# The first loads and constants of a decoder layer: two DMA queues, gains first, identity ahead of the zeroing

## What is computed

```python
def rms_norm(x, g):
    y = xf * lax.rsqrt(jnp.mean(xf * xf, axis=-1, keepdims=True) + EPS)
    return (y * g.astype(jnp.float32)).astype(x.dtype)

h = rms_norm(x, attn_norm_g)                 # x (1, 256, 2048)
proj = h @ w_in                              # (256, 11344)
(q_sb, k_sb, v_sb, q_ds, k_ds, v_ds, q_ix, k_ix, w_ix, g_sb, g_ds) = jnp.split(proj, IN_OFFSETS, axis=-1)
...                                          # two attentions, merged by gates
x = x + merged @ w_out
h = rms_norm(x, ffn_norm_g)
u = causal_depthwise_conv(h @ w_up, conv_w, conv_b)
gate, val = jnp.split(u, 2, axis=-1)
x = x + (jax.nn.silu(gate) * val) @ w_down
```

## Time and profile before

| | us |
|---|---|
| median of 3 runs | 1442.99 |
| lowest, highest | 1441.86, 1443.41 |
| the profiled execution, in all | 1443.47 |
| its span (first to last instruction) | 1441.7 |
| TensorE busy within the span | 1430.5 |
| VectorE, ACT, POOL busy | 1141.1, 841.9, 443.4 |

### The profile page before, as it was taken

How to read it: one execution, slowest core, us unless ns; L and a number is a source line. 1 busy time by engine, 2 the same in 40 slices (tenths; PEclk the granted TensorE clock), 3 DMA queues, 4 the chain that set the end, 5 groups by cost and what they waited for, 6 DMA issues and landing times.

```text
span 1441.7 us, 23615 instructions
## 1 busy us (share of the span) xinstructions
PE 1430.5 (99%) x7570; PEld 1224.0 (85%) x7570; DVE 1141.1 (79%) x1532; ACT 841.9 (58%) x1181; POOL 443.4 (31%) x487
## 2 busy tenths in 40 slices
PE   8999999999999999999999999999999999999999
PEld 7888888888888888888888888888888888788887
DVE  6778998986656556899967777778778778899988
ACT  6545677566767766666664555454554545465553
POOL 2310000423232213650015455755556555200000
PEclk9999999999999999999999999999999999999999
DMA  7555665655454545557555565555655565476564
GB/s 247 190 190 163 205 201 188 190 183 174 155 173 147 173 168 182 185 199 232 201 180 185 191 189 189 177 192 192 195 189 181 183 200 187 170 245 205 198 210 147
DMA packets 120535, 272.24 MB, mean 189 GB/s; under 512 B 10800, under 2 KB 10832, under 8 KB 120480
## 3 DMA queue, kind: packets, MB, share of 16 engines
q1 hardware_dynamic: 119424, 269.12, 56.9%
q0 software_dynamic: 736, 2.42, 0.6%
q10 hardware_dynamic: 320, 0.01, 0.0%
HBM read 269.42 MB, written 2.10 MB: 188 GB/s over the span
## 4 chain that ended last, share of the span: by engine, by line
PE 93%; DVE 3%; DMA 1%; issue 1%; POOL 1%; ACT 1%; DVEq 0%; ACTq 0%; POOLq 0%; SPq 0%
PE bank L2063 92%; DVE lo L1662 1%; DVE lo L1208 1%; PE bank L2112 1%; DMA raw<-in_w_out 0%; DMA raw<-in_w_down 0%; DMA rows_in<-in_attn_norm_g 0%; POOL u L2027 0%; ACT hi L719 0%; PE bank L2327 0%; PE bank L2368 0%; DVE conv L1614 0%; POOL conv L2030 0%; DVE y L1752 0%; DVE msum L1225 0%
## 5 line engine op out<-in xcount | busy, mean ns | idle before, releaser
L1099 DVE TENSOR_TENSOR lo<-raw,hi 128x1024 fp32r<-128x1024 f32 (+1 forms) x343 | 446.8, 1308 | 165.8 <-ACT hi L632 165.0
L632 ACT ACTIVATE hi<-raw 128x1024 fp32r<-128x1024 f32 (+1 forms) x343 | 360.1, 1053 | 271.6 <-PE bank L2063 267.5
L2063 PE MATMUL bank<-h2T,hi 128*128 128x512 f32 x1408 | 483.3, 394 | 0.0
L2063 PE MATMUL bank<-h2T,lo 128*128 128x256 f32 x1408 | 376.8, 278 | 0.0
L2063 PEld LDWEIGHTS bank<-h2T,hi 128*128 128x128 f32 x1408 | 257.9, 188 | 53.5
L2063 PE MATMUL bank<-hT,hi 128*128 128x512 f32 (+1 forms) x784 | 273.9, 396 | 0.0
L2063 PEld LDWEIGHTS bank<-h2T,lo 128*128 128x128 f32 x1408 | 264.4, 188 | 7.8
L2063 PE MATMUL bank<-hT,lo 128*128 128x256 f32 (+1 forms) x784 | 213.0, 282 | 0.0
L2027 POOL TENSOR_TENSOR u<-u,rms_row 128x256 f32<-128x256 f32 x88 | 120.8, 1373 | 198.7 <-DVE u L1604 179.7
L2063 PE MATMUL bank<-hi,ffT 128*128 128x512 f32 x576 | 177.6, 389 | 1.4 <-DVE lo L1662 1.4
L2063 PEld LDWEIGHTS bank<-hT,hi 128*128 128x128 f32 (+1 forms) x784 | 144.2, 187 | 29.7 <-DVE hT L1124 0.4
(11 more groups left out here) (297 smaller groups left out, 2018.4 us busy)
## 6 DMA issues: line engine op xcount, KB each, us to landing
raw<-in_w_up SPq DMA_DIRECT2D x176, 512.0 KB, 3.5
raw<-in_w_in SPq DMA_DIRECT2D x160, 512.0 KB, 3.4
raw<-in_w_down SPq DMA_DIRECT2D x88, 512.0 KB, 4.0
raw<-in_w_branch SPq DMA_DIRECT2D x32, 512.0 KB, 3.5
raw<-in_w_out SPq DMA_DIRECT2D x24, 512.0 KB, 4.6
raw4h<-in_w_in SPq DMA_DIRECT2D x8, 512.0 KB, 3.3
raw5h<-in_w_in SPq DMA_DIRECT2D x8, 512.0 KB, 4.0
y<-in_x SPq DMA_DIRECT2D x4, 512.0 KB, 6.8
```

Of the source, the lines that this page charges most:

```text
L632: act.activation(hi[s][:, 0:width], raw[s][:, 0:width], ACT.Copy)\
L1099: dve.tensor_tensor(lo[s][:, 0:width], raw[s][:, 0:width], hi[s][:, 0:width].bitcast(f32), ALU.subtract)\
L2063: return pe.matmul(o, l, r, start=start, stop=stop, skip_group_check=True)
```

## The change

Three things at the front of the program, and nothing behind it.

- x and the 80-column weights are issued by SP and ACT instead of SP alone. SP issues x(0,0), tile 1, x(1,0), tile 3. ACT issues x(0,1), tile 0, x(1,1), tile 2.
- ACT issues the gains of the attention norm as its first instruction. Row 0 of `rows_in` is no longer zeroed (only its first 16 partitions are read, and the load fills them), so that ACT need not wait for POOL. The two loads of positions now stand behind ACT's four new issues.
- POOL makes the identity first and zeroes `rows_in` after it, now 5 rows of 128 columns. TensorE waits for the identity alone ahead of its 14 transposes, and for the other mask later, ahead of L2159.

```diff
@@ -527,6 +527,19 @@
                 engine.wait_ge(w_used, end)
 
+        def load_x(engine, half, t):
+
+            cols = slice(half * BLOCK, (half + 1) * BLOCK)
+            engine.dma_start(y[:, t, cols], x[0, t * P:(t + 1) * P, cols])\
+                .then_inc(x_in[2 * half + t], 16)
+
+        def load_tail(engine, c):
+
+            rows = w_in[c * TAIL_CK * P:(c + 1) * TAIL_CK * P, TAIL_AT:TAIL_AT + TAIL]
+            engine.dma_start(raw[c][:, 0:TAIL_CK * TAIL].rearrange("p (k c) -> p k c", k=TAIL_CK),
+                             rows.rearrange("(k p) c -> p k c", p=P)).then_inc(w_landed[c], 16)
+
+
         @block.sync
         def _(sp):
             def load(slot, dst, src):
@@ -542,15 +555,10 @@
                          rows.rearrange("(k p) c -> p k c", p=P))
 
-            for half in range(2):
-                cols = slice(half * BLOCK, (half + 1) * BLOCK)
-                for t in range(TH):
-                    sp.dma_start(y[:, t, cols], x[0, t * P:(t + 1) * P, cols])\
-                        .then_inc(x_in[2 * half + t], 16)
-                for c in range(C_ROWS // 2 * half, C_ROWS // 2 * (half + 1)):
-                    rows = w_in[c * TAIL_CK * P:(c + 1) * TAIL_CK * P, TAIL_AT:TAIL_AT + TAIL]
-                    load(c, raw[c][:, 0:TAIL_CK * TAIL].rearrange("p (k c) -> p k c", k=TAIL_CK),
-                         rows.rearrange("(k p) c -> p k c", p=P))
+            load_x(sp, 0, 0)
+            load_tail(sp, 1)
+            load_x(sp, 1, 0)
+            load_tail(sp, 3)
             for b in range(2):
                 for g in range(2):
                     load_group(ROWS_AT[b] + g * CPG, w_in, 0,
@@ -649,11 +657,13 @@
                     act.activation(dst[:, kt, 0:S], bank[kt % 4][:, 0:S], ACT.Copy,
                                    scale=params[:, gain + kt:gain + kt + 1]).then_inc(xT_hi, 1)
 
-            prime(act, relu_done)
-
-            act.wait_ge(rows_zero, 1)
             act.dma_start(rows_in[0:KT, 0, :], attn_norm_g.rearrange("(t p) -> t p", p=P))\
                 .then_inc(small_in, 16)
+            load_x(act, 0, 1)
+            load_tail(act, 0)
+            load_x(act, 1, 1)
+            load_tail(act, 2)
+            prime(act, relu_done)
             for t in range(TH):
                 act.dma_start(pos_i[:, t:t + 1], positions[0, t * P:(t + 1) * P].unsqueeze(1))\
                     .then_inc(pos_in, 16)
@@ -1837,18 +1847,19 @@
 
         @block.gpsimd
         def _(pool):
-            pool.memset(rows_in[:, :, :], 0.0).then_inc(rows_zero, 1)
             pool.memset(ident[:, :], 0.0).then_inc(const_set, 1)
+            pool.memset(warm[:, :], 1.0).then_inc(warm_set, 1)
+            pool.wait_ge(const_set, 1)
+            pool.affine_select(out=ident[:, :], in_=ident[:, :], compare_op=ALU.not_equal,
+                               fill=1.0, base=0, pattern=[[-1, P]], channel_multiplier=1)\
+                .then_inc(const_sel, 1)
+            pool.memset(rows_in[:, 1:6, :], 0.0).then_inc(rows_zero, 1)
             pool.memset(neg_tri[:, :], -1.0).then_inc(const_set, 1)
             pool.memset(neg_one[:, :], -1.0).then_inc(const_set, 1)
             pool.wait_ge(const_set, 3)
-            pool.affine_select(out=ident[:, :], in_=ident[:, :], compare_op=ALU.not_equal,
-                               fill=1.0, base=0, pattern=[[-1, P]], channel_multiplier=1)\
-                .then_inc(const_sel, 1)
             pool.affine_select(out=neg_tri[:, :], in_=neg_tri[:, :], compare_op=ALU.is_ge,
                                fill=0.0, base=0, pattern=[[-1, P]], channel_multiplier=1)\
                 .then_inc(const_sel, 1)
-            pool.memset(warm[:, :], 1.0).then_inc(warm_set, 1)
 
             pool.wait_ge(rows_zero, 1)
             pool.dma_start(rows_in[0:KT, 1, :], ffn_norm_g.rearrange("(t p) -> t p", p=P))\
@@ -2130,7 +2141,7 @@
                 for _ in range(count):
                     pe.transpose(A[0][:, 0:P], ident[:, :], ident[:, :])
 
-            pe.wait_ge(const_sel, 2)
+            pe.wait_ge(const_sel, 1)
             keep_warm(14)
             pe.wait_ge(small_in, 16)
             pe.transpose(A[3][:, 0:KT], rows_in[0:KT, 0, :], ident[0:KT, 0:KT])\
@@ -2154,6 +2165,7 @@
                     i = mm(A[2][0:TAIL, 0:S], wl[:, j, :], hT[:, kt, 0:S], False, kt == KT - 1)
                 i.then_inc(w_used, 1)
 
+            pe.wait_ge(const_sel, 2)
             pe.wait_ge(conv_in, 16 * 3)
             pe.wait_ge(params_done, 1)
             pe.transpose(A[3][:, KT:2 * KT], rows_in[0:KT, 1, :], ident[0:KT, 0:KT])
```

## The result

The changed kernel's median is 1445.91 us (1443.78 to 1449.56), that of the kernel before, run beside it, 1443.43 (1441.86 to 1444.44), 22 runs each. The ratio is 1.0016, with a 95% interval of 1.0010 to 1.0022: 2.3 us slower, and outside the range that was given, whose upper end was 1444.6. The ratio and its interval are worked out from the single runs, so the ratio need not be the quotient of the two medians.

The account below looks back on a forecast made before the run. TensorE, busy 99% of the span, was taken to bound the kernel, so only closing up the front could help. The terms -0.1 -0.3 +0.1 gave -0.3 us, 1442.7 against a median of 1442.99; range 1440.8 to 1444.6.

Parts of the forecast that it names:

- What bounds the kernel: TensorE, busy 99% of the span; a shift of the front before 19.56 us should reach the end one for one.
- The two gates: TensorE's waits in the front: at 6.90 us for the gains, with x(0,1) close behind, and at 13.00 for x(1,1).
- x and the 80 columns over two queues: Loads at the front: no gain from the second queue; first real transposes at about 6.8 instead of 6.90, 0.1 us gained.
- x(0,1) held up by 0.1 us: First gate: a tile of columns beside x(0,1) delays it by about 0.1 us if packets alternate, 0.56 if it goes ahead.
- ACT's issues hidden: ACT's 7 issues before its table load, 0.42 to 0.53 us each, all over by 6.0, needed at 7.17; cost 0.
- Positions behind x, 0.9 us at x(1,1): Second gate: x(1,1) lands up to 0.9 us earlier, at 12.1; 0.3 us gained, bounds 0 and 0.92.
- The clock, 0.1 lost, bounds 0 and 0.3: First tiles of x: a longer TensorE idle stretch after earlier warm-up transposes may leave the clock low; 0.1 us lost.
- a low clock later than 12.7: Sign of a wrong forecast: TensorE's granted clock 0.50 after 12.7 us, adding up to 1 us not counted.
- B: Rival: two queues move x faster, opening the first gate 0.8 us earlier; 1.7 us gained in all, 1441.3; chance 0.10.
- C: Rival: x(0,1) shares the engines, lands at up to 8.1, TensorE starts 1.3 us later; 1444.3; chance 0.15.
- x(0,1) after 7.2: Sign at the first gate: x(0,1) landing after 7.2 us would show the forecast wrong and the slower rival C right.

Follow-up runs that it names:

- before_12_more: Kernel before, with 12 more transposes of the identity behind TensorE's wait for x(1,0) and x(1,1); 1444.77 us, ratio 1.0008.
- before_24_more: Kernel before, with 24 more transposes of the identity behind TensorE's wait for x(1,0) and x(1,1); 1445.95 us, ratio 1.0019.
- swap_tiles: Changed kernel with tiles 0 and 1 of the 80 columns exchanged between the queues, so SP issues tile 0; 1443.96 us, ratio 1.0005 to before.
- after_third: The changed kernel measured a third time, without an edit; 1445.43 us, ratio 1.0012 to the kernel before.
- x_only_on_act: Changed kernel with ACT issuing only the gains, x(0,1) and x(1,1), SP the rest and then the positions; 1444.07 us, ratio 1.0004 to before.
- positions_on_sp: Changed kernel with the two loads of positions issued by SP behind its four instead of by ACT; 1445.91 us, ratio 1.0011 to before.
- undo_queues: Changed kernel with SP issuing all eight transfers of x and the 80 columns in the old order; 1444.01 us, ratio 0.9998 to before.
- gains_only: Changed kernel with SP issuing all eight transfers again and POOL's old order, TensorE waiting for both masks; 1443.79 us, ratio 1.0001 to before.
- before_positions_last: Kernel before, with the two loads of positions issued by SP behind its eight; 1443.09 us, ratio 0.9996.
- x_beside_x: Changed kernel with x(1,0) and x(0,1) each second in their queue, tile 0 behind x(1,0), positions behind SP's four; 1445.16 us, ratio 1.0007 to before.

## Why the prediction was wrong, point by point

*What bounds the kernel.* Right, as far as the medians tell: one for one is what a shift in front costs (before_12_more, before_24_more). The two gates were read rightly, and that x(0,1) is next behind the gains. The third thing that TensorE needs in the front, tile 0, I did not look at, since it had 1.3 us of cover before: landed at 7.8, taken by ACT at 9.05. That is the step that failed: in "*x and the 80 columns over two queues*" the tiles stand only as something that may hold up x(0,1), and nobody asks when they land themselves. Moving tile 0 from third place behind two tiles of x to the other queue, beside x(1,0), cost it 3.8 us. Of these the kernel lost 1.6 by the ratios of the changed kernel and swap_tiles; by the profiles 0.8 (dense at 20.82 for 20.00), and 2.0 where the clock was low in both (after_third's 22.43 for x_only_on_act's 20.39).

*x(0,1) held up by 0.1 us.* Measured 1.2 (7.91 for 6.68), of which TensorE's start saw 1.0. The sum counted bytes at a fixed rate. From 2 to 5 us the engines moved 225 GB/s at the same share of 0.90 where they had moved 295, from 5 to 7 us 266 where they had moved 153 at 0.71 (first two rows: after; last: before).

```profile
2.00:5.00 3.00, 3.00 (x15) 2.61 (x13) 0.00 (x0) 0.00 (x0) 2.92 (x8) 1.00 0.90 225
5.00:7.00 2.00, 0.05 (x1) 0.00 (x0) 0.00 (x0) 0.00 (x0) 2.00 (x21) 1.00 0.95 266
...
5.00:7.00 2.00, 1.13 (x6) 0.75 (x5) 0.00 (x0) 0.00 (x0) 2.00 (x21) 1.00 0.71 153
```

From 2 to 7 us both kernels moved 1.2 MB. The second queue lost no bytes over that time: it changed their order, with tile 1's packets among those of x(0,1) instead of behind them. The term was also set against the wrong row: 6.90 is the transpose of the gains, those of x begin at 7.06.

*ACT's issues hidden.* Wrong in size: the term was 7 issues of 0.42 to 0.53, over by 6.0; the last two took 3.24 together and the table load ended at 8.31. It happened to end together with x(0,1), and positions_on_sp shows that it cost nothing that can be measured.

*Positions behind x, 0.9 us at x(1,1).* In the changed kernel x(1,1) landed at 13.09, later than before. Where the positions alone were moved it was 0.3 to 0.5. That they slow the stretch of the earlier trace rows was right (275 GB/s without them for 148). That the whole 0.9 us reaches x(1,1) was not.

*The clock, 0.1 lost, bounds 0 and 0.3.* The early end of the warm-up transposes costs nothing measurable (undo_queues against gains_only). The bounds were set for one place, and the low clock struck at another: behind the wait for tile 0, where it can add 1.5 to 1.6 us to the front (22.43 for 20.93 and 20.82). The prediction's own sign for this, a low clock later than 12.7, is seen there and in positions_on_sp, not in the first profile, where the clock is up again at 11.85.

*The rivals.* B did not happen: by x(0,1) and the GB/s above the second issuer saved less than nothing. The Trainium skill, "DMA: Bandwidth & Descriptors", section "Issuing engines are not separate DMA queues", which leaves several issuers no more than the issue time, was right against B; it says nothing of a loss, and here there was one. C named the right direction, and its sign, x(0,1) after 7.2, came true: it was late by 1.2, near its 1.4. But that was not the main victim. The price that C gave is 1.3 over the median it went by; x(0,1) alone is worth 0.7 and 0.6 us (swap_tiles and x_only_on_act, where it was as late, by their ratios, 1.3 either way). The chance of C, 0.15, rested on x(0,1) sharing first with x(0,0), which is needed at the same time; but what stood beside it was tile 1, in flight from 1.3 to 8.3 while x(0,1) was from 1.3 to 7.9; x(0,0) had landed at 5.0.

*The range.* Its upper end was C plus 0.3. (Its lower end holds a slip: half the spread of 1.6 us is 0.8, not 0.5. It had no part in the miss.) No case combined a late x(0,1), a late tile and a low clock, though one edit can bring all three.

## What to carry to other kernels

When transfers are moved to another queue, list every consumer in the order in which the engines want it, with its landing and its slack before, and ask of each one what will stand beside it: count its packets and not only its bytes. Tile 0 has a third of the bytes of a tile of x and four times its packets; beside one and POOL's loads it took 9.8 us, where it had taken 6.0 in one queue with the tiles of x. Put what is wanted first into one queue in that order. And when an issuer gets more to issue ahead of its own work, take the price of an issue from a moment at which that much is already outstanding, not from the first issues.

## What the hardware showed that I had not expected

- An issue that comes behind enough others stalls its issuer: the sixth and seventh issue of ACT took 3.24 us together (3.04 and 3.17 in the two other profiles), where the same two take 0.85 as ACT's second and third (undo_queues, from 1.34 on). SP stalls likewise: its ninth and tenth, the positions in before_positions_last, took 3.46 us from the start of the one to the end of the other, and its sixth in x_only_on_act took 3.14 alone, while in the kernel before none of its first eight took over 0.65. So it isn't the number of issues that decides; what does, no run here tells.
- The bytes moved at the same busy share depend on which packets are under way. At a share of 0.90 it was 295 GB/s with x in one queue and 225 with x and a tile of small packets in two, both from 2 to 5 us. From 5 to 7 us, with mostly tiles of x in both queues, x_beside_x moved 393 at 1.03. So two queues are not slower as such.
- The same POOL instruction at the same place took 0.45 us in one profile of before and 1.43 in the other. Their POOL timelines, first and second profile (start, length; the one ahead of it has the same shape and took 1.44 in both):

```profile
260.21 1.44 POOL L1878 TENSOR_TENSOR rot_d<-qn,sin_d 128x128 f32<-128x128 f32 x1
261.62 0.45 POOL L1880 TENSOR_TENSOR rot_d<-qn,sin_d 128x128 f32<-128x128 f32 x1
```

```profile
261.53 1.44 POOL L1878 TENSOR_TENSOR rot_d<-qn,sin_d 128x128 f32<-128x128 f32 x1
262.94 1.43 POOL L1880 TENSOR_TENSOR rot_d<-qn,sin_d 128x128 f32<-128x128 f32 x1
```

  The second also starts the sequence 1.3 us later. Both together make the wait of TensorE at 264 us. What goes with the length is VectorE. When the short one starts, at 261.62, VectorE is idle; when the long one starts, at 262.94, it is in the middle of its work (VectorE's rows, first and second profile):

```profile
262.28 1.69 DVE L1099 TENSOR_TENSOR lo<-raw,hi 128x1024 fp32r<-128x1024 f32 x1 [0.95 <-ACT hi L632]
...
257.83 6.23 DVE L1099 TENSOR_TENSOR lo<-raw,hi 128x1024 fp32r<-128x1024 f32 x4
```

  It is so in all 20 profiles: in 11 VectorE is idle when the instruction starts and it takes 0.45 to 0.47 us, in 9 VectorE is in a `tensor_tensor` and it takes 1.43 to 1.50. The later stages, from the dense stream to the end, take 1422.2 us in the mean of the 11 and 1423.7 in that of the 9, a difference of the size of the scatter between runs. Both kinds stand among the kernels with a late tile 0 (5 and 3) and among the others (6 and 6). No run moves VectorE's work on purpose, so this is seen and not tested.
